# One decoder layer in float32 on one core: the first norm, the first input products and the fill products of the RWKV stage are put in another order

## What is computed

```
h = [meta; x]
n = h * rsqrt(mean(h*h) + 1e-6) * norm1_g
u = n @ w_in            # 1280 "shift" columns, then q, k, v of two attentions, then 3 x 1024 gate columns
shift columns: u + (previous row - u) * mu, then RWKV-7 time mixing (6 heads of 64)
rest: stick-breaking attention (5 heads), forgetting attention (5 heads)
h = h + (sum of the three mixers, projected and gated) @ w_out
h = h + MoE(RMSNorm(h))  # top-1 group of 4, top-2 experts inside it
return h[16:]
```

## Time and profile before

| | |
|---|---|
| median of three runs | 930.11 us (929.64 to 930.9) |
| the profiled execution's own time | 930.29 us |
| its span in the profile | 928.5 us |
| PE busy with matmuls | 884.8 us, 95% |
| DVE, ACT, POOL busy | 285.6, 196.6, 100.0 us |
| mean granted TensorE clock | 0.986 of full |

### The profile page before, as it was taken

One profiled execution on the slowest core, in us unless ns is written; L12 is line 12 of the kernel. 1 busy time (PEld: TensorE's weight loads), 2 busy tenths in 40 slices (PEclk: granted clock), 3 DMA queues, 4 the chain that ended last, 5 costly groups with the idle time before them and its releaser, 6 DMA issues.

```text
span 928.5 us, 16339 instructions
## 1 busy us (share of the span) xinstructions
PE 884.8 (95%) x6978; PEld 509.1 (55%) x6978; DVE 285.6 (31%) x587; ACT 196.6 (21%) x390; POOL 100.0 (11%) x225
## 2 busy tenths in 40 slices
PE   3999999999998999999999999999999998999995
PEld 2878888877776765445454444444445563333331
DVE  3244810312312321452312244333531143222212
ACT  5134101122016111132302111135002220111100
POOL 7720000000003200002000000000000001221121
PEclk9999999999999999999999999999999989999998
DMA  8212127000000000037121113015555068899972
GB/s 230 59 47 81 56 71 204 2 2 3 2 2 1 2 3 25 24 92 194 46 63 28 45 46 85 8 53 199 171 223 238 23 261 306 310 382 385 385 267 109
DMA packets 76136, 109.77 MB, mean 118 GB/s; under 512 B 16892, under 2 KB 61068, under 8 KB 71969
## 3 DMA queue, kind: packets, MB, share of 16 engines
q1 hardware_dynamic: 71296, 93.22, 29.5%
q0 software_dynamic: 4768, 15.52, 5.8%
HBM read 100.32 MB, written 10.50 MB: 119 GB/s over the span
## 4 chain that ended last, share of the span: by engine, by line
PE 91%; DVE 2%; DMA 2%; ACT 2%; issue 1%; SPq 0%; DVEq 0%; POOL 0%; POOLq 0%; ACTq 0%
PE ps L1489 19%; PE ps L1514 10%; PE ps L1847 9%; PE ps L1466 8%; PE ps L1433 8%; PE ps L1793 6%; PE ps L1754 5%; PE ps L1873 5%; PE ps L1471 4%; PE ps L1669 1%; PE ps L1737 1%; PE ps L1834 1%; PE ps L1711 1%; PE ps L1661 1%; PE ps L1687 1%
## 5 line engine op out<-in xcount | busy, mean ns | idle before, releaser
L1489 PE MATMUL ps<-arena 128*128 128x512 f32 x304 | 142.6, 606 | 0.0
L1489 PEld LDWEIGHTS ps<-arena 128*128 128x128 f32 x304 | 54.7, 191 | 62.8 <-issue 60.9
L1514 PEld LDWEIGHTS ps<-arena 64*64 64x64 f32 x2376 | 73.3, 134 | 23.7 <-issue 13.7
L1847 PE MATMUL ps<-arena 128*32 128x512 f32 x624 | 84.9, 592 | 0.5 <-DVE arena L1292 0.5
L1514 PE MATMUL ps<-arena 64*64 64x64 f32 x2376 | 80.3, 220 | 1.6 <-ACT arena L780 1.3
L1433 PE MATMUL ps<-arena 128*128 128x264 f32 x320 | 74.5, 392 | 0.6 <-PE ps L1433 0.6
L1433 PEld LDWEIGHTS ps<-arena 128*128 128x128 f32 x320 | 61.0, 192 | 13.3 <-issue 1.7
L1466 PE MATMUL ps<-arena,h 128*128 128x264 f32 x256 | 65.5, 397 | 0.5 <-PE ps L1433 0.5
L1793 PE MATMUL ps<-arena 128*128 128x512 f32 x128 | 56.2, 594 | 0.0
L1754 PE MATMUL ps<-yT_all,arena 128*128 128x512 f32 x112 | 51.9, 616 | 2.1 <-DMA arena<-in_w_p_fox 1.9
L1466 PEld LDWEIGHTS ps<-arena,h 128*128 128x128 f32 x256 | 45.9, 188 | 9.5 <-issue 0.8
(11 more groups left out here) (344 smaller groups left out, 1036.2 us busy)
## 6 DMA issues: line engine op xcount, KB each, us to landing
arena<-in_moe_w_down SPq DMA_DIRECT2D x32, 512.0 KB, 14.7
arena<-in_moe_w_gate SPq DMA_DIRECT2D x13, 1024.0 KB, 11.3
arena<-in_moe_w_up SPq DMA_DIRECT2D x13, 1024.0 KB, 15.1
arena<-in_w_in SPq DMA_DIRECT2D x19, 512.0 KB, 3.9
arena<-in_w_in SPq DMA_DIRECT2D x5, 1024.0 KB, 9.6
h<-in_x SPq DMA_DIRECT2D x8, 512.0 KB, 5.1
arena<-in_w_out SPq DMA_DIRECT2D x1, 4096.0 KB, 12.8
h<-in_w_in SPq DMA_DIRECT2D x3, 1024.0 KB, 5.3
```

The lines of the kernel that those rows point to most:

```text
L1489: ins = mm(ps[:, gate_bank(n), :], weights_of_gate(n)[:, c, :], nT[:, c, META:L], start=(c == 0), stop=(c == DC - 1))
L1514: ins = mm(psf[q, 512 * bank + c * CH:512 * bank + (c + 1) * CH], lhs(q, c), rhs(q, c), start=True, stop=True)
L1847: ins = mm(ps[rs, bank, :].rearrange("p (h n) -> p h n", h=2), xgT[:, s, c, rs], w1[ws][:, :, c, :], start=(c == 0), stop=(c == DC - 1))
```

## The change

SP and the norm:

```diff
+            sp.dma_start(h[:, 0, :], x[0:P, :]).then_inc(sem("tile_in0"), 16)
             sp.dma_start(metax[0:META, :], meta).then_inc(sem("meta_in"), 16)
-            for t in range(NT):
+            sp.dma_start(g1c, g1.rearrange("(c p) -> p c", p=P)).then_inc(sem("g1_in"), 16)
+            for t in range(1, NT):
                 sp.dma_start(h[:, t, :], x[t * P:(t + 1) * P, :]).then_inc(sem(f"tile_in{t}"), 16)
-            sp.dma_start(g1c, g1.rearrange("(c p) -> p c", p=P)).then_inc(sem("g1_in"), 16)
...
-            for i in range(RING):
-                load_piece(i)
+            load_piece(0)
```

```diff
+            def root(ss, rows):
+                done(a.activation(ss, ss, ACT.Ln, scale=1.0 / D, bias=eps_c[0:rows]))
+                done(a.activation(ss, ss, ACT.Exp, scale=-0.5), "rstd_ready")
...
+            dve.wait_ge(sem("meta_in"), 16)
+            done(tt(squares, metax[0:META, :], metax[0:META, :], ALU.mult))
+            done(v.tensor_reduce(stat[0:META, 4:5], squares, mybir.AxisListType.X, ALU.add), "ss_ready")
             for t in range(NT):
+                dve.wait_ge(sem("rstd_ready"), t + 1 if t == 0 else t + 2)
+                done(ts(xs[:, t, :], h[:, t, :], stat[:, t:t + 1], None, ALU.mult), "xs_ready")
                 if t == 0:
+                    dve.wait_ge(sem("rstd_ready"), 2)
+                    done(ts(metax[0:META, :], metax[0:META, :], stat[0:META, 4:5], None, ALU.mult), "xs_ready")
+                    dve.wait_ge(sem("g1_in"), 16)
+                if t >= 1:
+                    chunks_out(t - 1, DC)
+                if t == 1:
+                    dve.wait_ge(sem("xT_psum"), 2)
                     done(tt(nT[:, :, 0:META], ps[:, 7, 0:DC * META].rearrange("p (c n) -> p c n", c=DC), gain(DC, META), ALU.mult), "nT_meta")
+            chunks_out(NT - 1, T_SPLIT)
```

PE (WARM = 18; `turned(t)` is the eight transposes of a tile, `shift_half(n, hf)` the eight products of half hf of chunk n):

```diff
+            for _ in range(WARM):
+                mm(ps[:, 5, 0:P], ident[:], ident[:], start=True, stop=True)
...
+            turned(0)
+            pe.wait_ge(sem("xs_ready"), 2)
...
+            turned(1)
+            pe.wait_ge(slot_sem(0), landed[0])
+            pe.wait_ge(sem("nT_low"), 2)
             pe.wait_ge(sem("nT_meta"), 1)
+            shift_half(0, 0)
+            turned(2)
+            turned(3)
+            shift_half(1, 0)
+            pe.wait_ge(sem("nT_low"), 4)
+            pe.wait_ge(sem("nT_high"), 1)
+            shift_half(0, 1)
+            shift_half(1, 1)
```

```diff
-                    if k == 1:
-                        fill_qkv(2)
...
-                fill_qkv(3)
+                fill_qkv(TURN_FILL)
...
                     units(4 + 2 * (k % 2), cm(lhs), cm(rhs)).then_inc(sem("g_psum"), 1)
-                    fill_qkv(1)
                 fill_qkv(INIT_FILL)
```

More of the change, by code:

```diff
@@ L42 @@
 RING = 3
+WARM = 18
 RING_W = FW + FH
@@ L56 @@
 SHIFT_ORDER = (4, 1, 2, 0, 3)
-INIT_FILL = 4
+PARAMS_A, PARAMS_B = 16 * 8, 16 * 14
+INIT_FILL = 9
+TURN_FILL = 5
 LEVEL_FILL = 3
@@ L323, in hybrid_layer @@
             for k_ in range(4):
-                pe_order.append((("tr", p_, k_), {1: 2, 3: 3 + 5}.get(k_, 0)))
+                pe_order.append((("tr", p_, k_), TURN_FILL if k_ == 3 else 0))
             pe_order.append((("init", p_), INIT_FILL))
@@ L535, in _ @@
                 masked(incl_st[q, :], 1.0, ALU.is_ge, [[1, CH]], 0, -1)
+            done(g.memset(reset[:], 1.0))
+            done(g.memset(reset[:, 0:L:CH], 0.0), "consts_ready")
             for lv in range(6):
@@ L767, in _ @@
             done(a.activation(stat[:, 8:9], stat[:, 0:1], ACT.Copy), "act_phase")
+            act.wait_ge(sem("g1_in"), PARAMS_B)
+            done(a.mul(qg8, qgc, 0.125))
             while DC * (out_n[0] + 1) <= HEAD_FILL:
@@ L942, in _ @@
             ts, tt, stt = v.tensor_scalar, v.tensor_tensor, v.scalar_tensor_tensor
+            done(v.memset(eps_c, EPS), "ms_ready")
             for j in range(SC):
                 done(v.memset(U[:, j, 0:1], 0.0))
[L946 to L949, removed]
@@ new lines, in chunks_out @@
+            def chunks_out(t, c1):
+                dve.wait_ge(sem("xT_psum"), t + 1 if t == 0 else t + 2)
+                done(tt(nT[:, 0:c1, META + t * P:META + (t + 1) * P],
+                        psf[:, 1024 * t:1024 * t + c1 * P].rearrange("p (c n) -> p c n", c=c1), gain(c1, P), ALU.mult), "nT_low")
+            squares = tmp_shift[0:META, :, :].rearrange("p a b -> p (a b)")[:, 0:D]
+            dve.wait_ge(sem("meta_in"), 16)
+            done(tt(squares, metax[0:META, :], metax[0:META, :], ALU.mult))
@@ L1384, in _, with turned @@
             pe.wait_ge(sem("ident_ready"), 1)
[L1385 to L1390, removed]
+            for _ in range(WARM):
+                mm(ps[:, 5, 0:P], ident[:], ident[:], start=True, stop=True)
+            def turned(t):
+                pe.wait_ge(sem("xs_ready"), 1 if t == 0 else t + 2)
                 if t == NT - 1:
@@ L1421, in _ @@
             for i in range(N_SHIFT):
-                pe.wait_ge(slot_sem(i), landed[i])
-                w = slot(i)
+                if i >= 1:
+                    pe.wait_ge(slot_sem(i), landed[i])
                 for j in range(2):
@@ L1426, in _ @@
                         pe.wait_ge(sem("chunk_out"), n - 1)
[L1427 to L1435, removed]
+                        shift_half(n, 0)
+                        shift_half(n, 1)
                     if 2 <= n <= 4:
```

80 lines of the change are left out of this document (39 added, 41 removed).

## The result

The changed kernel takes **917.01 us** (median of 4 runs, 915.25 to 917.33), against 929.88 for the kernel before in the same session (4 runs, 925.28 to 930.9): ratio 0.9867, interval [0.9832, 0.9902]. The forecast was 918.8, with 916.0 to 922.4 as its range. The profiled execution took 916.74, its span is 915.0 (930.29 and 928.5 before), its mean granted clock 0.988 (0.986).

The account below looks back on a forecast made before the run. PE was taken as the bound (busy 884.8 of 928.5 us), except at the start, bound by loads, ACT and DVE. -6.0 and -5.4 make -11.4 from 930.29: 918.9, predicted as 918.8; range 916.0 to 922.4.

Parts of the forecast that it names:

- The start: Up to the end of chunk 1: 33.0 instead of 39.04, -6.0 us, 1.4 from the low clock gone, 4.6 from order.
- meta sums on DVE through: DVE, before scaling tile 0: the meta rows' product (1.23) and sum (about 1.27) are through at about 7.25.
- unread products end: PE's start: 18 products whose results nothing reads begin at 1.4, last about 7 us and end at 8.4.
- low half of chunk 0: PE's first eight real products, from 14.8: 3.57 us.
- tiles 2 and 3 turned: PE's transposes between chunk 0's first eight products and the next 24: 3.9 us, twice 1.97.
- The first rival: PE's start: the clock falls all the same, costing 1.4 to 3.4 us; total 920.2 to 922.2; chance 0.18.
- The third rival: SP's queue: pieces 1 and 2 land late behind eight small loads and the kernel ends slower; landing at 48 gives 934; chance 0.02.
- The fills: Fill products between 64x64 units in three head pairs: 15 lumps removed save 5.1, covering PE's mask wait 0.28; -5.4 us.
- a break: Switch between 64x64 units and a fill lump: each removed saves 0.34, 0.15 in the units and 0.19 in the lump.
- The second rival: Head pairs: joined fills give little, DVE's mask sets the G batches' pace; only 2.0 of 5.4 come, 922.2; chance 0.12.
- the margins: Head pairs: ACT's copy and DVE's mask fit under one batch with 0.18 and 0.29 left, less the signal's way back.
- allowance for the router: Router's 1.2 GHz stretch, 750 to 756: may fall on other work, 1.6 better to 1.8 worse; taken as 0.

Follow-up runs that it names:

- e2: The changed kernel with the fill lumps of before, so the new start alone: 920.34 us, ratio 0.9911.
- e6: The changed kernel with POOL's table `reset` written at its old place, behind the level masks: 914.63 us, measured once.
- e1: The kernel before with only the fill edit, lumps joined among the G products and between the transposes: 922.54 us, ratio 0.9937.
- e11: The kernel before with only the lumps of the G products joined, those of 2 and 3 between the transposes left: 924.07 us, ratio 0.9963.
- e8: e7 with three unread products ahead of tile 1's transposes and six behind them: 912.97 us, ratio 0.9843.
- e7: The changed kernel with the meta rows loaded ahead of tile 0 and DVE moving tile 1 before scaling tile 2: 915.21 us, ratio 0.9864.
- e3: The changed kernel without the 18 unread products at the start: 917.46 us, ratio 0.9881.
- e4: The changed kernel with more unread products: 24 at first, 2 ahead of tile 1's transposes, 6 behind them: 913.24 us, ratio 0.9857.
- e9: e8 with weight piece 0 issued ahead of tiles 2 and 3: 912.21 us, ratio 0.9831.
- e10: e8 without the six unread products behind tile 1's transposes; the three ahead of them stay: 914.05 us, ratio 0.9854.
- e5: The changed kernel with the meta rows loaded ahead of tile 0: 914.9 us, ratio 0.9857.
- e12: e10 with 12 unread products at the start instead of 18: 912.06 us, ratio 0.9836.

## Why the prediction was right

**The start, -6.0 predicted, -5.78 measured,** but out of wrong terms that cancel, and with luck: e2 and e6 have the same start and end chunk 1 at 34.82 and 34.73, which would be -4.2 and -4.3. The start of the kernel before varies too: at the head pairs e1 and e11, which do not touch it, are 0.61 and 1.36 ahead.

| step | predicted | measured |
|---|---|---|
| tile 0 there | 4.6 | 5.3 |
| meta sums on DVE through | 7.25 | 8.39 |
| unread products end | 8.4 | 7.35 |
| tile 1 turned | 13.4 | 13.71 |
| first product | 14.8 | 15.48 |
| low half of chunk 0 | 3.57 | 5.32 |
| tiles 2 and 3 turned | 3.9 | 1.75 |
| last 24 products | 10.7 | 10.71 |
| end of chunk 1 | 33.0 | 33.26 |

- *The meta rows.* "Right behind" tile 0 was wrong by a microsecond: 64 KB behind a tile landed 4.58 after issue, where alone in front they take 2.1 (e8). The prices of DVE's two steps (1.23 and 1.27) were right, 1.23 and 1.22.
- *DVE's list.* The prediction counted tile 1's move as 1.25 after its transposes. It did not count what stands ahead of it: the move of tile 0, the meta columns and the scaling of tile 2, so that DVE started that move at 14.15 though PE was done at 13.71. e7 shows its size.
- *Transposes.* The prediction read 1.97 as a transpose batch's price at any clock ("the same 1.97 at 0.50"). It is the price at 1.2 GHz; at 2.4 GHz it is 1.04 to 1.09. In the kernel before three of the four batches ran at 1.2 GHz, two of them (3.81 for both, from 12.13) under a recorded 1.00 (e3 shows why that is no measurement); the one at 18.33 took 1.15. The changed kernel's tiles 2 and 3 take 1.75 for both, which gave 2.15 back.
- *The clock.* The prediction went by the row of PEclk 1.00 from 0. The Trainium skill, "TensorE: Matmul & The Clock Gate", Part 1, that the array is throttled until activity releases it, was right, and e3's durations show it. The first rival (the clock falls all the same) came true in the changed kernel, by its own sign, a PEclk of 0.50 between 10 and 30, and with gaps of up to 1.87, where the prediction had none over 1.5. It cost 1.75 on the low half; 0.9 on tile 1's transposes (1.97 for 1.09) delayed nothing, since DVE began its move only at 14.15, 0.44 after they ended. In e2 and e6 it cost 3.1 and 3.3 on the low half. The forecast's time was right all the same, since the forecast had charged tiles 2 and 3 at the low clock's price without knowing it. With the clock kept through the low half (e4) the start gives 7.43.
- *SP's queue.* Pieces 1 and 2 were issued at 14.91 (predicted: by about 13) and landed 5.7 and 8.2 us after their issue; PE asked at 33. The third rival is dead. One small load alone, w0, held the queue for 5.03.

**The fills, -5.4 predicted, -4.57 measured.** The mechanism was right and 0.34 a break was too much for 12 of the 15: the 0.15 in the units was taken from one pair of batches, 2.25 for 1.20, and is 0.105 in a row of five; with 0.19 a break is 0.295 (e11). The three in the transposes are 0.34. So the term is 12 x 0.295 + 3 x 0.34 + 0.28 = 4.84, against 4.95 in e1. The 0.38 between e1 and the changed kernel are the pause of the list (4.59 for 4.21). The second rival is dead: no wait took the breaks' place. DVE idles 0.29 to 0.39 before each mask, so the margins were as thin as worked out and held.

**What the sum did not have.** Of 13.5 in the span the two parts account for 10.35. With these alone the profiled 930.29 would have become 919.9, 1.1 above the forecast and still in its range; what brought it down to 916.74 was not in the sum. The time behind the three head pairs is 604.4 in the profile of before, the longest of all fourteen, 601.25 in the changed kernel and 597.7 to 603.2 in the other twelve. In the rest, the landing of one later weight took 5.75 after issue where 6.96 stood, worth 1.2, and PE's wait for it went from 0.5 (e9) to 1.9 (before) among these kernels; and the low-clock stretches after 400 us, the tail aside, came to 13.7 us in the kernel before and 10.2 in the changed one, half of which difference, 1.7, is time. The fourteen profiles have between 0 (e6) and 13.7 us of such stretches, at 458 to 504, at 640 and at 733 to 769, and the kernel before alone ran from 924.11 to 930.9 over these sessions. So one execution of before was profiled on its worse side. The medians differ by 12.9, 2.5 more than the parts; whether a change of order shifts these stretches in the mean stays open. The prediction's allowance for the router (-1.6 to +1.8) is of that size.

## What to carry to other kernels

Check the clock by durations (here a transpose of 128x128 in eight: 1.97 or 1.09) before a row of granted clock near the start is believed, and price each operation at the clock of the stretch where it will run. Unread products help where they fill the gap in which the clock falls, not where PE idles longest: the eighteen at the beginning raised the clock (the rate doubles at 4.95) but did not keep it, and three more in the right place kept it (e10 against e7, 30.18 against 32.87 at the end of chunk 1). Whether those three alone would do was not tried. On an engine with one list, write out everything that stands ahead of the step that releases the bound; and of a repeated saving take the marginal price in the longest joined row.

## What the runs showed of the hardware that was not expected

- The recorded clock is 1.00 until PE's rate first doubles, whatever the real rate is (e3: products at 0.44 an instruction until about 21, then 0.22).
- The switch from 64x64 units to 128x128 products and back costs 0.295 us a break (0.19 and 0.105).
- A load of 64 KB takes 2.1 us to land when issued first and 4.6 behind one of 512 KB; the vector w0, 1.5 KB in 4-byte runs, held SP's queue for 5.03 (3.64 before, 6.08 in e8), where k_a, as long, took 0.49.
- PE can pause up to 1.5 us at a fixed number of its list while the DMA engines are busy (e4: 148.43 to 155.48 for the G products that take 5.58 elsewhere), and goes on 2.49 to 2.65 after a packet of the instruction queue starts. A few instructions more or fewer at the start move its place 140 us later. It cost 0 in e5 and e12 and 1.24 in e10.
